# ScalarE makes the attention's diagonals, and the rotary sum of q and k moves onto TensorE

## What is computed

```python
def token_mixers(h, ...):
    z = h @ w_in
    aq, ak, av, bx, bg, cq, ck, cv, gl = jnp.split(z, points, axis=-1)
    ya = chunk_band_attention(aq, ak, av, rel_bias)         # 8 heads, softmax, bias by distance
    yb = rglru_block(bx, bg, ...)                           # convolution, gated scan
    cq, ck = apply_rope(cq, cos, sin), apply_rope(ck, cos, sin)
    yc = diff_attention(cq, ck, cv, lam, lam_init, subln_g) # per head: p0 - lam * p1
    ...
def apply_rope(t, cos, sin):
    t1, t2 = t[..., :half], t[..., half:]
    return jnp.concatenate([t1 * c - t2 * s, t2 * c + t1 * s], axis=-1)
def peer_ffn(h, w_q, sub_keys, u, v):
    ...                                                     # top 16 of the product keys, 8 heads
    hid = jax.nn.gelu(jnp.einsum('td,thkd->thk', xb, u[experts]))
    return jnp.einsum('thk,thkd->td', g * hid, v[experts])
```

## Time and profile before

| | us |
|---|---|
| median of 3 runs | 3905.95 |
| the three runs | 3897.07, 3905.95, 3914.15 |
| the profiled execution | 3898.55 |
| its span, first to last instruction | 3896.7 |
| PE busy | 2408.7 (62%) |
| DVE busy | 2923.2 (75%) |
| ACT busy | 531.2 (14%) |
| POOL busy | 2397.6 (62%) |

### The profile page before, as it was taken

How to read it: one execution, slowest core, us unless ns; L and a number is a source line. 1 busy time by engine, 2 the same in 40 slices (tenths; PEclk the granted TensorE clock), 3 DMA queues, 4 the chain that set the end, 5 groups by cost and what they waited for, 6 DMA issues and landing times. The chain is left out here.

```text
span 3896.7 us, 29311 instructions
## 1 busy us (share of the span) xinstructions
PE 2408.7 (62%) x8928; PEld 1667.8 (43%) x8928; DVE 2923.2 (75%) x5647; ACT 531.2 (14%) x1237; POOL 2397.6 (62%) x2052
## 2 busy tenths in 40 slices
PE   8899527786798617767598717687788815600000
PEld 6676412464585313345486413355576513200000
DVE  2311786788877896778888797788777797798889
ACT  2310001122211101112110101122210101100000
POOL 0000377776675677766676577776566577777775
PEclk9989769997798859888698958998799968955555
DMA  4234699999899889999899989999799988999998
GB/s 176 96 107 140 213 324 361 369 392 348 294 408 409 339 316 347 368 384 392 325 389 409 352 321 347 361 390 391 291 365 409 370 323 308 355 350 367 368 387 339
DMA packets 359900, 1295.78 MB, mean 333 GB/s; under 512 B 40512, under 2 KB 40768, under 8 KB 359744
## 3 DMA queue, kind: packets, MB, share of 16 engines
q0 software_dynamic: 294912, 1073.87, 72.9%
q1 hardware_dynamic: 64256, 217.94, 14.8%
q10 hardware_dynamic: 576, 2.10, 0.1%
HBM read 1291.65 MB, written 2.10 MB: 332 GB/s over the span
## 5 line engine op out<-in xcount | busy, mean ns | idle before, releaser
L1057 POOL DMA_INDIRECT ring<-in_peer_u,eidx x1024 | 1222.6, 1194 | 960.1 <-DVE eidx L1181 475.1
L1057 POOL DMA_INDIRECT ring<-in_peer_v,eidx x1024 | 1174.8, 1147 | 516.8 <-issue 288.1
L1094 DVE CUSTOM_DVE_ANT_0 ring<-ring,hp 128x1024 f32<-128x1024 f32 x1024 | 1236.4, 1224 | 266.0 <-DMA ring<-in_peer_u,eidx 254.1
L1099 DVE SCALAR_TENSOR_TENSOR acc<-ring,wgt,acc 128x1024 f32<-128x1024 f32 x744 | 949.2, 1290 | 123.4 <-DMA ring<-in_peer_v,eidx 101.2
L519 PE MATMUL bank<-xt,panel 128*128 128x256 f32 x4096 | 952.8, 392 | 33.7 <-ACT raw L854 8.5
L519 PEld LDWEIGHTS bank<-xt,panel 128*128 128x128 f32 x4096 | 804.1, 198 | 164.0 <-issue 27.0
L752 PE MATMUL bank<-ring,dg 128*128 128x512 f32 x1120 | 549.6, 632 | 497.2 <-ACT dg L826 363.7
L752 PEld LDWEIGHTS bank<-ring,dg 128*128 128x128 f32 x1120 | 208.9, 198 | 825.4 <-issue 578.6
L594 PE MATMUL bank<-dg,ex 128*128 128x128 f32 x640 | 112.8, 349 | 149.2 <-DVE dg L1341 84.5
L594 PEld LDWEIGHTS bank<-dg,ex 128*128 128x128 f32 x640 | 105.4, 257 | 161.3 <-issue 145.7
L715 PE MATMUL bank<-yt,panel 128*128 128x256 f32 x768 | 173.6, 379 | 0.0
(11 more groups left out here) (164 smaller groups left out, 1884.0 us busy)
## 6 DMA issues: line engine op xcount, KB each, us to landing
panel<-in_panels SPq DMA_DIRECT2D x368, 512.0 KB
ring<-in_peer_u,eidx POOLq DMA_INDIRECT x1024
ring<-in_peer_v,eidx POOLq DMA_INDIRECT x1024
work<-in_rel_bias SPq DMA_DIRECT2D x16, 512.0 KB
gb<-in_ln_g SPq DMA_DIRECT2D x8, 512.0 KB
gb<-in_ln_b SPq DMA_DIRECT2D x8, 512.0 KB
panel<-in_keys SPq DMA_DIRECT2D x16, 256.0 KB
work<-in_x SPq DMA_DIRECT2D x4, 512.0 KB, 5.2
```

The lines of the kernel that those rows point to most:

```text
L1057: pool.indirect_dma_start(ring[:, n % RING, :], None, t_in["peer_u" if kind == "U" else "peer_v"], bass.IndirectOffsetOnAxis(ap=eidx[:, t, ...
L1094: v.tensor_tensor_reduce(row, row, hp[:, t, :], 1.0, 0.0, ALU.mult, ALU.add, hid[:, t, c:c + 1]).then_inc(used, 1)
L1099: stt(out=acc[:, t, :], in0=row, scalar=wgt[:, t, c:c + 1], in1=acc[:, t, :], op0=ALU.mult, op1=ALU.add).then_inc(used, 1)
```

## The change

ACT writes the four diagonals of a unit, where DVE did; DVE only makes the reciprocals, and in C scales the two of the second map by the factor that holds minus lambda. The rotation is computed as ident·(raw·cos) + swap·(raw·sin'), summed by PE in bank 1: DVE makes both products ahead, PE runs two matmuls where it ran one, and ACT copies the sum out as q and k. The signs of the sine table change places. Stage B no longer holds a permutation for unit 0: its turn stands ahead of the scores in stage C.

```diff
-            def swap_qk(s, u):
+            def turn_qk(s, u):
                 n = s * UNITS + u
-                pe.wait_ge(qk_ev["C"], n + 1)
+                pe.wait_ge(rot_done, n + 1)
                 if u >= 2:
                     pe.wait_ge(o_ev["C"], n - 1)
-                mm(bank[1][:, :], swap, raw[:, u % 2].rearrange("p a t -> p (a t)"), start=True, stop=True
-                   ).then_inc(swapped, 1)
+                mm(bank[1][:, :], ident, rot[:, 0].rearrange("p a t -> p (a t)"), start=True, stop=False)
+                mm(bank[1][:, :], swap, rot[:, 1].rearrange("p a t -> p (a t)"), start=False, stop=True
+                   ).then_inc(turned, 1)
...
+            def take_rope(s, u):
+                n = s * UNITS + u
+                act.wait_ge(turned, n + 1)
+                copy(qt[:, u % 2, :], bank[1][:, 0:HALF])
+                copy(kt(s % 2, "C", u), bank[1][:, HALF:2 * HALF]).then_inc(rope_done, 1)
+
...
+            def diagonals(kind, s, u):
+                n = s * UNITS + u
+                for i in range(4):
+                    if i % 2 == 0:
+                        act.wait_ge(rinv_done[kind], n * 2 + i // 2 + 1)
+                    fn(dg[:, u % 2 * 4 + i, :], ident, ACT.Copy, scale=rinv[:, u % 2, i:i + 1]).then_inc(dg_done[kind], 1)
 
...
                 take_v("C", s)
+                take_rope(s, 0)
                 exps("C", s, 0)
                 for u in range(UNITS):
+                    diagonals("C", s, u)
                     take_weighed("C", s, u)
+                    if u + 1 < UNITS:
+                        take_rope(s, u + 1)
                     gelus((s, "C", u, 4))
...
-                tt(rot[:, 0], raw[:, u % 2], cs[:, 0, half].unsqueeze(1).broadcast_to(wide), ALU.mult).then_inc(*own.one())
-                dve.wait_ge(swapped, n + 1)
-                tt(rot[:, 1], bank[1][:].rearrange("p (a t) -> p a t", a=2),
-                   cs[:, 1, half].unsqueeze(1).broadcast_to(wide), ALU.mult).then_inc(*own.one())
-                step()
-                tt(qt[:, u % 2, :], rot[:, 0, 0, :], rot[:, 1, 0, :], ALU.add).then_inc(*own.one())
-                tt(kt(s % 2, "C", u), rot[:, 0, 1, :], rot[:, 1, 1, :], ALU.add).then_inc(rope_done, 1)
-                dve.wait_ge(rope_done, n + 1)
-                step()
+                if n:
+                    dve.wait_ge(turned, n)
+                for a in range(2):
+                    ins = tt(rot[:, a], raw[:, u % 2], cs[:, a, half].unsqueeze(1).broadcast_to(wide), ALU.mult)
+                ins.then_inc(rot_done, 1)
...
-            def diagonals(kind, s, u):
+            def inverses(kind, s, u):
                 n = s * UNITS + u
                 for m in range(2):
+                    cols = rinv[:, u % 2, 2 * m:2 * m + 2]
                     dve.wait_ge(e_done[kind], n * 4 + m * 2 + 2)
...
+                    if kind == "C" and m == 1:
+                        v.reciprocal(cols, esum[:, u % 2, 2 * m:2 * m + 2]).then_inc(*own.one())
+                        step()
+                        ts(cols, cols, small[:, 13:14], None, ALU.mult).then_inc(rinv_done[kind], 1)
+                    else:
+                        v.reciprocal(cols, esum[:, u % 2, 2 * m:2 * m + 2]).then_inc(rinv_done[kind], 1)
```

More of the change, by code:

```diff
@@ L326, in trunk @@
         h_turned = sem("h_turned")
-        swapped = sem("swapped")
+        turned = sem("turned")
+        rot_done = sem("rot_done")
         s_done = {k: sem(f"s_done_{k}") for k in "AC"}
@@ L365, in trunk @@
         smax = {k: sem(f"smax_{k}") for k in "AC"}
+        rinv_done = {k: sem(f"rinv_done_{k}") for k in "AC"}
         dg_done = {k: sem(f"dg_done_{k}") for k in "AC"}
@@ L678, in stage_c @@
                 pe.wait_ge(ri_act, (s + 1) * 2)
+                turn_qk(s, 0)
                 scores("C", s, 0)
@@ L897, in stage_a @@
                 for u in range(UNITS):
+                    diagonals("A", s, u)
                     take_weighed("A", s, u)
@@ L1353, in attention_stage @@
                     maxima(kind, s, u)
-                    diagonals(kind, s, u)
+                    inverses(kind, s, u)
                     if kind == "C" and u + 1 < UNITS:
@@ L1499, in _constants @@
     c[:, C_FREQ] = (10000.0 ** (-(2.0 * (r % 32)) / HEAD_DIM)).astype(np.float32)
-    c[:, C_SIGN] = np.where(r < 32, -1.0, 1.0)
+    c[:, C_SIGN] = np.where(r < 32, 1.0, -1.0)
     c[:, C_EPS1] = 4.0 * EPS
```

12 lines of the change are left out of this document (1 added, 11 removed).

## The result

The changed kernel takes 3932.72 us, the median of 20 runs (3912.26 to 3963.89). The kernel before takes 3907.38 in 20 runs beside it (3886.02 to 3923.73). The ratio is 1.0071, with a 95% interval of 1.0054 to 1.0087: slower by 0.71%, some 28 us (the two medians themselves lie 25.3 apart). Forecast were 3926, between 3900 and 3956. The profiled execution of the changed kernel took 3934.64 us with a span of 3932.8.

A forecast was written before the change was run, and what follows sets the result against it. PE was taken to bound phase 0's attention and DVE to arrive last at C's hand-overs in phases 1 to 3; 15.7 + 6.3 - 1.7 = +20.3 us on the median of 3905.95 gave 3926, range 3900 to 3956.

The forecast's parts named there:

- Phase 0, stage A: PE waits before each weighing for ACT's diagonals, queued behind its copies or output: +0.7, +1.6, +1.6, +1.7, sum +5.6 us.
- Phase 0, stage C: Four diagonals, longer turn and eviction on PE's path: +2.7, +0.9, +2.4, +2.4 and +1.7 for units 0 to 3 and end; +10.1 us.
- The fifth: Phase 0, stage C, behind unit 3: its weighing waits for ACT's diagonals as in stage A, +1.7 us.
- Phases 1 to 3, stage A: PE's chain is late, so ACT's queue adds to it: 2.5 us each in phases 1 and 3, 1.3 in phase 2; +6.3.
- unit 2's: Stage A of phases 1 and 3: diagonals on ACT lengthen the chain at unit 2 by +0.6 us.
- Phases 1 to 3, stage C: Unit 0 loses 3.7 us three times (+11.1), hand-overs between units gain 12.8; sum -1.7 us.
- the nine hand-overs: Stage C, phases 1 to 3, unit to unit: scores ready earlier for DVE, 1.6 us gained at eight, none at one; -12.8.
- The wait in front of the maxima: Stage C, phases 1 to 3: DVE's wait moves from the products to before the maxima, still some 6 us long.
- rival 1: Added gaps lower PE's clock, in phase 0 projections, scores and weighing: 14 and 6 us more, 3946; chance 0.20.
- rival 2: Phases 1 to 3 delays partly swallowed by stages waiting for transfers: 12 to 15 us less left, about 3912; chance 0.23.
- rival 3: DVE's relief decides at the nine hand-overs in C: 7 us each, 63 in all, 3876; chance 0.07.
- the condition: Forecast called wrong if phase 0's span grows by less than 10 or more than 25 us.

The follow-up runs named there:

- products ahead of the rows: Changed kernel with DVE's two products of unit 0 in stage C ahead of the twelve expert rows there: 3933.11 us, ratio 1.0052 to before.
- A's diagonals back: Changed kernel with stage A's diagonals written by DVE again, those of stage C still on ACT: 3913.20 us, ratio 0.9994 to before.
- no rows in A: Changed kernel with stage A's 76 expert rows per phase moved to stage G: 4164.56 us, ratio 1.0652; same move in the kernel before: 4134.85 us, 1.0578.
- the rotation alone: Kernel before with only the rotation changed (two products, two matmuls, ACT's copy), DVE still writing the diagonals: 3904.53 us, ratio 0.9988.
- diagonals alone: Kernel before with only the diagonals moved to ACT and the rotation untouched: 3963.26 us, ratio 1.0134.
- scores ahead: Rotation change only, unit 0's products ahead of its rows, plus next unit's scores ahead of the weighing in both attention stages: 3947.16 us, ratio 1.0085 to before.
- the wait alone: Kernel before, where in stage A ACT also writes four unread squares and PE's weighing waits for them: 3924.31 us, ratio 1.0014.
- diagonals earlier: Changed kernel with ACT's diagonals of the next unit ahead of its copies of q and k instead of behind: 3935.81 us, ratio 1.0053 to before.

## Why the prediction held, and where it did not

**Phase 0, stage A: right to the decimal.** 0.7, 1.6, 1.6 and 1.7 forecast; 0.66, 1.65, 1.65 and 1.7 measured, in four kernels. At units 1 and 2 the copies of q and k ahead of two diagonals are the whole of it; with the diagonals ahead of the copies it is 0.

**Phase 0, stage C: 7.3 for 10.1.** Four of the five terms hold within 0.35 us. The fifth, +1.7 behind unit 3, came out as -1.2, and G and O, forecast at nothing, at -2.5. Both go with the clock: between the maxima of unit 3 and the norm PE of the kernel before was at its low level for 24 us, that of the changed one for 10. From the first maxima of unit 3 to the norm, before and then after:

```profile
204.74:385.44 180.70, 171.61 (x724) 137.54 (x723) 21.55 (x59) 21.23 (x49) 0.00 (x0) 0.93 0.38 124
```

```profile
220.12:397.15 177.03, 166.23 (x724) 133.47 (x724) 20.69 (x57) 22.24 (x53) 0.00 (x0) 0.97 0.39 127
```

That the sum came out so low is luck of this profile. Three other kernels run the same code in this stage and phase (products ahead of the rows, A's diagonals back, no rows in A). In all three units 2 to 3 take 20.6 us and not 17.4, as here with the products ahead:

```profile
200.99:221.62 20.63, 17.90 (x71) 13.27 (x72) 3.19 (x10) 5.88 (x22) 0.00 (x0) 0.83 0.16 52
```

From unit 0's first maxima to the norm the changed kernel's profile is 2.1 us longer than that of before; theirs are 3.9, 4.9 and 8.9 longer. The terms after unit 0 had 7.4.

**Phases 1 to 3, stage A: the step that was mis-sized.** 6.3 forecast, 23.5 in the profile. Where ACT's queue was what I priced, the terms hold: unit 1 was put at +0.9 and is +0.7 in all three phases, unit 3 at +0.2 and is +0.2 to 0.3 in phases 1 and 3. The term that was mis-sized is unit 2's: +0.6 forecast for phases 1 and 3, +4.8 and +5.6 measured, and +3.9 to +6.7 in the three other kernels whose A diagonals ACT writes. I priced the chain and not what the weighing meets while gathers run: PE's results come late there and its clock falls behind them, 3.4 to 10.2 us of low level in units that had none. The remaining 8.7 stand at unit 0 in phase 3, where a kernel without the move has them too. The trace of before had such late releases (a copy that followed PE's records by 7.0 us in A of phase 2), and the sum has no term for them.

**Phases 1 to 3, stage C: right.** Unit 0 at +3.6, +3.6, +2.4 for +3.7; the nine hand-overs -1.7 on average for -1.6, and the one in phase 2 for which I took nothing gained too. The chain behind unit 3 got 0.8 to 1.2 longer, where I had written 0: four diagonals on ACT in front of the last weighing can be a part of it, but not the whole, since the rotation alone, with DVE writing them, has +0.9 there in phases 1 and 3.

**The wait in front of the maxima** was named and then priced at nothing. It was the largest thing to be had in these runs: rows moved into it are worth 39 us.

**The rivals.** The clock (rival 1) decided part of it in A of phases 1 and 3, behind late releases. In phase 0 the changed kernel's profile spent even less time at the low level, but the three others of the same code lost 3.2 us to it from unit 2 to 3 of C, so the rival was real there too. That the transfers swallowed a part (rival 2) has no sign in the profiles: the stages T moved by +3.4, -4.0 and +0.8. DVE's relief (rival 3) did not decide. Phase 0 grew by 11.7 us at the norm, within the 10 to 25 named as the condition.

**How much of the number was luck.** The path was right: the cost stands on PE's path in phase 0 and at unit 0 of C, the gain in C's hand-overs. The total of 28 us for 20 stayed inside the range although one stage came out 17 us over its term in the profile. Phase 0 and the stages G and O were 5.2 under theirs, C's hand-overs 2.4 better, and the upper end of the range had been drawn for a fall of the clock in phase 0.

A rule was weighed in the prediction: the Trainium skill ("ScalarE: Activation LUTs", Rules for kernel authors) sends a plain multiply to VectorE, 15 us by the two durations. The runs agree with it on the side, and not on the reason: the operation's own speed costs nothing in phase 0 where it stands early (the gap of 0 above), and in the whole the bill was 30 us in A alone and 52 for the diagonals without the rotation.

**What stays open.** Why PE's releases come late, and why they are most frequent in the kernel with the diagonals alone (58 us) and in the one with the scores ahead (77). Shown is that they need rows and gathers beside them: none in phase 0, none in A without rows (that move took away both, DVE's row work and the transfers, so which of them it is isn't shown). Some come and go from one profile to the next: the copy of v in A of phase 2 comes 7.0 late before and 7.7 after, and in time with the wait alone; that of phase 3 is 5.8 late after and in time before. The one at unit 2 of A in phases 1 and 3 stays with ACT's diagonals, and what links them is open. That the two parts of the change don't add up is part of the same question.

## What to carry to other kernels

Before work goes to an idle engine, look at what stands in front of it in that engine's queue at that moment: here 1.3 us of work behind a copy that waits for a projection cost PE 1.65 us a unit in phase 0, and none when it stood ahead of it. In phases with gathers beside it the same shift won nothing, so it has to be measured there. Apply a change of two parts one by one: the good half (rotation, with its products early) was hidden behind the bad one. And where the busiest engine waits at a fixed place in every round, move its independent work into the wait; it brought more than any shorter chain tried here, and it did not set off the losses of the reordering of PE.

## What the runs showed of the hardware

- While gathers fill the DMA engines (1.0 busy, over 400 GB/s, around the late ones), semaphores of PE can come 9.4 us (diagonals alone, A of phase 2) and once 14.2 us (scores ahead, C of phase 2) after its last record has ended. In one stretch the groups of a weighing, 28 records, were released 2.6, 6.2, 11.2 and 14.8 us after its start, about 0.6 us a record from the second group on, where records stand at 0.13. In phase 0, without gathers, the same waits end 0.04 us after the last record on average.
- The granted clock fell from 2.4 to 1.2 GHz 2.7 us after PE's last record before such a wait and stayed there 10.2 us, into the next unit's weighing, whose 28 records then took 5.9 us instead of 3.6.
- A gap of 2 us on PE at the same place in phase 0 is followed by a low level in some kernels and not in others: unit 3's stretch in C takes 17.4 us at 1.00 in the changed kernel and 19.5 at 0.82 with the diagonals earlier, which has the smaller gaps. Even the same code does both: 17.4 at 1.00 in the changed kernel and 20.6 at 0.83 in three kernels with the same stage.
- Of six kernels in which DVE writes A's diagonals and four in which ACT does, only the four have the late weighing of unit 2 in phases 1 and 3: 8.8 to 11.4 us from its first record to the end of ACT's last copy of it, for 4.2 to 6.2 in the six.
